# Upper products first, then lower ones, in each half chunk of a split fp32 matmul stream

## The reference

```python
proj  = rms_norm(x, ln_mix_pre) @ w_in            # 45 chunks of 128 output channels
x    += rms_norm(mixed @ w_out, ln_mix_post)      # 16
u     = conv(rms_norm(x, ln_ffn_pre) @ w_ffn_up)  # 4 x 22
f     = (gelu(gate) * up) @ w_ffn_down            # 4 x 16, over 11 tiles each
p     = rmsnorm(x, norm1_w) @ w_in_2              # 42
x    += mixed_2 @ w_out_2                         # 16
q     = rmsnorm(x, norm2_w) @ w_pq                # 16
act   = gelu(h @ u_tab.T) * gate_of_expert        # 8 x 16
x    += act @ v_tab                               # 8 x 16
```

## Time and profile before

| what | value |
|---|---|
| time, median of 3 runs | 4353.81 us (4353.56 to 4356.52) |
| profiled execution: its own time, its span | 4359.34 us, 4357.4 us |
| TensorE busy | 3741.0 us, 86% |
| VectorE busy | 2529.6 us, 58% |
| ScalarE busy | 1609.8 us, 37% |
| mean granted TensorE clock | 0.894 |
| data moved | 597.59 MB, mean 137 GB/s |

### The profile page before, as it was taken

The page is one execution under the profiler, slowest core; times in us unless marked ns, Lnnn a source line. Parts: engine busy times, 40 slices in busy tenths (PEclk is TensorE's granted clock), DMA queues, the critical chain, the costliest instruction groups (busy, mean ns, idle before and its releaser), DMA issues.

```text
span 4357.4 us, 73593 instructions
## 1 busy us (share of the span) xinstructions
PE 3741.0 (86%) x25038; PEld 3179.9 (73%) x25038; DVE 2529.6 (58%) x4253; ACT 1609.8 (37%) x2407; POOL 79.0 (2%) x80
## 2 busy tenths in 40 slices
PE   7996899999997977566766686379999999999998
PEld 5874778888886863455555575268888888888887
DVE  3465576767666753433233457976656566565565
ACT  3443344444443432211111232134445444354453
POOL 0000000000000000001000000000000000000000
PEclk8996999999998985667667797699999999999999
DMA  5550445555553530000000143146566565665654
GB/s 172 188 169 1 154 144 181 181 186 176 191 183 123 186 116 3 8 9 6 5 28 2 58 147 114 55 167 212 184 211 208 186 210 185 206 210 186 209 188 138
DMA packets 166055, 597.59 MB, mean 137 GB/s; under 512 B 18304, under 2 KB 26624, under 8 KB 164672
## 3 DMA queue, kind: packets, MB, share of 16 engines
q1 hardware_dynamic: 159456, 559.10, 39.1%
q0 software_dynamic: 6496, 36.96, 2.3%
HBM read 574.76 MB, written 20.97 MB: 137 GB/s over the span
## 4 chain that ended last, share of the span: by engine, by line
PE 81%; DVE 12%; issue 3%; ACT 2%; DMA 1%; DVEq 1%; SPq 0%; ACTq 0%; POOL 0%; POOLq 0%
PE bank L480 44%; PE bank L482 22%; PE bank L732 9%; PE bank L503 1%; DVE hot_row L1996 1%; PE bank L720 1%; PE bank L694 1%; DVE inv_T L1821 1%; DVE quad L1386 1%; PE bank L710 0%; PE bank L746 0%; DVE q_ms L1695 0%; DVE h_two L1376 0%; DVE rb L1371 0%; DVE inv_T L1807 0%
## 5 line engine op out<-in xcount | busy, mean ns | idle before, releaser
L480 PE MATMUL bank<-h_two,w_hi 128*128 128x512 f32 x5616 | 1974.5, 396 | 55.0 <-DVE h_two L1376 30.4
L482 PE MATMUL bank<-h_two,w_lo 128*128 128x256 f32 x5616 | 1582.2, 282 | 0.0
L1339 DVE TENSOR_TENSOR w_lo<-raw,w_hi 128x1024 fp32r<-128x1024 f32 (+1 forms) x1086 | 1262.4, 1186 | 98.7 <-ACT w_hi L968 94.7
L968 ACT ACTIVATE w_hi<-raw 128x1024 fp32r<-128x1024 f32 (+1 forms) x1086 | 1077.2, 1025 | 571.2 <-PE bank L482 496.7
L480 PEld LDWEIGHTS bank<-h_two,w_hi 128*128 128x128 f32 x5616 | 1060.3, 189 | 301.9 <-issue 38.2
L482 PEld LDWEIGHTS bank<-h_two,w_lo 128*128 128x128 f32 x5616 | 1071.3, 191 | 0.0
L480 PE MATMUL bank<-p_two,w_hi 128*128 128x512 f32 x2048 | 717.9, 393 | 0.0
L482 PE MATMUL bank<-p_two,w_lo 128*128 128x256 f32 x2048 | 572.5, 280 | 0.0
L480 PEld LDWEIGHTS bank<-p_two,w_hi 128*128 128x128 f32 x2048 | 383.8, 187 | 91.8
L482 PEld LDWEIGHTS bank<-p_two,w_lo 128*128 128x128 f32 x2048 | 384.2, 188 | 0.0
L973 ACT ACTIVATE stage<-bank 128x256 f32<-128x256 f32 x258 | 99.0, 384 | 581.2 <-PE bank L482 579.8
(11 more groups left out here) (329 smaller groups left out, 3202.1 us busy)
## 6 DMA issues: line engine op xcount, KB each, us to landing
raw<-in_u_tab SPq DMA_DIRECT2D x256, 512.0 KB, 4.2
raw<-in_v_tab SPq DMA_DIRECT2D x256, 512.0 KB, 4.5
raw<-in_w_up SPq DMA_DIRECT2D x176, 512.0 KB, 4.3
raw<-in_w_in SPq DMA_DIRECT2D x174, 512.0 KB, 4.5
raw<-in_w_out SPq DMA_DIRECT2D x64, 512.0 KB, 4.3
raw<-in_w_down SPq DMA_DIRECT2D x64, 512.0 KB, 3.5
raw<-in_w_pq SPq DMA_DIRECT2D x32, 512.0 KB, 4.7
gates<-g_stage POOLq DMA_DIRECT2D x8, 2048.0 KB, 7.5
```

What stands on the lines that cost most here:

```text
L480: nc.tensor.matmul(o[:], wh, two[:, k, :, :].rearrange("p a t -> p (a t)"), start=(k == 0), stop=False)
L482: last = nc.tensor.matmul(o[:, T:2 * T], wl, two[:, k, 0, :], start=False, stop=(k == nk - 1))
L968: nc.scalar.activation(w_hi[c % 2][:, at:end], raw[c % 2][:, at:end], ACT.Copy).then_inc(hi_done, 1)
L1339: nc.vector.tensor_tensor(w_lo[c % 2][:, at:end], raw[c % 2][:, at:end], w_hi[c % 2][:, at:end].bitcast(F32), ALU.subtract).then_inc(lo_do ...
```

## The change

In each half chunk the upper products of all its tiles come first, behind a wait for `hi_done` alone. The lower products of the same tiles follow, behind the wait for `lo_done`. `per_tile` is called ahead of the upper product. `half_done` is counted up by the last lower product of the half, as before. The number of products, their operands and the engines' other queues stay as they are.

```diff
-                for k in range(nk):
-                    if k * P in (0, HALF):
-                        pe.wait_ge(lo_done, it * 4 + (2 * c + 1 + k * P // HALF))
-                    if per_tile:
-                        per_tile(k)
-                    wh, wl = w_hi[c % 2][:, k * P:(k + 1) * P], w_lo[c % 2][:, k * P:(k + 1) * P]
-                    nc.tensor.matmul(o[:], wh, two[:, k, :, :].rearrange("p a t -> p (a t)"),
-                                     start=(k == 0), stop=False)
-                    last = nc.tensor.matmul(o[:, T:2 * T], wl, two[:, k, 0, :], start=False, stop=(k == nk - 1))
-                    if (k + 1) * P == HALF or k == nk - 1:
-                        last.then_inc(half_done, 1)
+                for part, ks in enumerate((range(HALF // P), range(HALF // P, nk))):
+
+                    pe.wait_ge(hi_done, it * 4 + (2 * c + 1 + part))
+                    for k in ks:
+                        if per_tile:
+                            per_tile(k)
+                        nc.tensor.matmul(o[:], w_hi[c % 2][:, k * P:(k + 1) * P],
+                                         two[:, k, :, :].rearrange("p a t -> p (a t)"), start=(k == 0), stop=False)
+                    pe.wait_ge(lo_done, it * 4 + (2 * c + 1 + part))
+                    for k in ks:
+                        last = nc.tensor.matmul(o[:, T:2 * T], w_lo[c % 2][:, k * P:(k + 1) * P], two[:, k, 0, :],
+                                                start=False, stop=(k == nk - 1))
+                    last.then_inc(half_done, 1)
```

## The result

| what | before | after |
|---|---|---|
| time, median (lowest to highest) | 4355.17 us (4353.56 to 4359.34, 4 runs) | 4384.73 us (4384.21 to 4386.45, 4 runs) |
| profiled execution: its own time, its span | 4359.34 us, 4357.4 us | 4384.72 us, 4382.7 us |
| mean granted TensorE clock | 0.894 | 0.892 |

The ratio is 1.0067, with a 95% interval of 1.0050 to 1.0085: slower, by 29.6 us on the medians and 25.4 us between the two profiled executions. The forecast was 4360 with a range of 4343 to 4405. That range held. The forecast's own one, 4355 to 4364, did not: the sign was as forecast, the size that of rival 1. By the forecast's own measure (8.7 us) this is slower, which it had given 0.38 against 0.46 for no change.

What follows compares the result with a forecast made beforehand. TensorE, busy 86% of the span, was taken as the bound, mostly by `chunk`'s products. Terms 6.4 + 0.9 + 0.5 + 0.5 + 0.4 - 2.4 = +6.3 us on the 4353.8 median gave 4360 us, range 4343 to 4405.

Steps and rivals of the forecast that it cites:

- rival 1: Pairs of `chunk` dearer in groups: 4407 if the slow rate rules, 4385 at 3 ns per lower; chance 0.26.
- No change of the products: Steady state of `chunk`: an upper and lower pair costs the same when eight uppers, then eight lowers follow; 0 us.
- The bounds (-226 and +611): All 8368 pairs: -226 us if 27 ns excess came from alternating, +611 if loads of 0.19 us paced lower runs.
- Rival 2: Pairs of `chunk` cheaper in groups: 4318 at 5 ns a pair, 4134 at all 27; chance 0.12.
- The two rates: Stages of `chunk` run at 0.3467 or about 0.353 us a pair; redrawn, all fast -8.6 us, all slow +47.
- The extra waits: Two more waits per chunk, 1086 in all, in TensorE's queue: 0 us taken, 35 us if uncovered.
- The `p_two` wait: First `p_two` chunk of 8 groups: eight lowers queue behind the wait at tile 15, 8 x 0.80 = +6.4 us.
- Rival 4: The `p_ready` loss at first `p_two` chunks does not come: 4353.7, no change; chance 0.12.
- `f_two`, `w_lo`: Two lowers stuck behind each of four `f_two` stops, +0.9 us; two `w_lo` waits let subtraction start earlier, -2.4 us.
- Rival 3: Waits for VectorE (`w_lo`) were the point: 4341.5 if all 12.3 us went and no `p_ready` loss came; chance 0.02.
- Stage starts: Lowers deferred behind `h_two` waits: first output +0.5, second output +0.5, FFN and second input +0.4 us together; query none.

Runs made afterwards that it cites:

- the split one: Changed kernel, but tile 15 taken alone in the second half of each group's first `p_two` chunk: 4376.77 us, against 4383.55 for the changed kernel.

## Why the prediction was off in size

**No change of the products, "I take 0 for this term": the step that failed.** Grouped pairs are dearer than the fast alternating ones: (2793 - 2773)/8 = 2.5 ns in `h_two` stages and (2827 - 2800)/8 = 3.4 ns in `p_two` ones. In the expert part that is the 10.7 us that the run with only steady chunks grouped shows. The bounds (-226 and +611) held it, and rival 1 had named its size (3 ns, 4385), but put it down to missed loads. The traces do not decide on that reason. Loads can come 0.11 us apart and lowers stand 0.120 apart, so missed loads alone do not give the number; but only those lowers are dearer whose own weights had no upper to load under, and at 384 columns the step is gone. That 4385 stands so near the measured 4384.73 is luck: it needs 25 us from dearer pairs, and the steady chunks of the two traces differ by 11.0 (10.3 + 8.3 - 5.1 - 2.5), since part of before ran at the slow rate. The first chunks differ by 14.4 (6.7 + 7.7) where the forecast had 6.3. Rival 2 is refuted: grouped pairs are not cheaper, and a product in a run of its kind keeps 13 to 17 ns above its columns (230 for 512 columns, 213 by the clock; only the first lower of a run has 7). By the Trainium skill ("TensorE: Matmul & The Clock Gate", section "Back-to-back issue gap") a pair would be 325 ns. The section gives this gap for an isolated product and says that a stream of loads and products is spaced otherwise. The grouped runs show 349, so its few nanoseconds do not hold here in either order.

**The two rates.** The prediction bounded this by -8.6 and +47 us. The changed kernel shows no second rate in the traces: all `h_two` stages run at 2793, between 2773 and 2827. So it lost 20 ns per half where before had been fast and won 34 where it had been slow. The slow rate may be why before scatters over 18 us (4347.15 to 4365.16 in 23 runs) and the changed kernel over 2 to 6; with one trace of before, that is not shown. The trace of the run with two waits and alternating products had the first input stage slow and the first output stage fast, the reverse of the trace of before, so it is not tied to a stage. The median loss of 29.6 us exceeds the 25.4 of the traces because the profiled execution of before was 4.2 us above its median.

**The extra waits.** 0 forecast, ratio 1.0002 measured, in the alternating order. Right.

**The `p_two` wait.** 8 x 0.80 = 6.4 us forecast. The first `p_two` chunk took 0.83 us more in each of 8 groups, 6.7 us, and taking tile 15 out of the group gave 6.8 us back. Right, by its mechanism as well: the profile counts the wait as 0.6 us (4.9 for 8) from the modelled end of upper 14, but upper 15 was due at 3183.07 + 7 x 0.23 = 3184.68 and started at 3185.48, 0.8 us later. The forecast's own terms add up to 3175.27 + 0.1 + 0.23 + 0.94 = 3176.54, 0.75 us late and not 0.80, a slip of 0.4 us in all. Rival 4 is out.

**`f_two`, `w_lo`.** `f_two` waits grew by 0.7 us, and the first down chunks by 0.65 in all, for 0.9 forecast; the subtraction's two waits shrank by 3.0 us for 2.4. Both right. Rival 3 is out.

**Stage starts.** +1.4 us forecast for the output, FFN and second input stages. Measured, with the work ahead of each, +1.4 (first output), +5.1 (FFN), +1.9 (second input), -2.1 (second output). The FFN start shows why. The windows of TensorE there, before and then after (us, busy and count, granted clock, DMA share, GB/s):

```profile
522.00:532.00 10.00, 7.01 (x32) 1.00 0.34 107
540.00:550.00 10.00, 8.86 (x32) 0.81 0.00 0
...
561.00:570.00 9.00, 8.46 (x48) 1.00 0.00 0
```

```profile
522.00:532.00 10.00, 9.57 (x31) 0.69 0.32 107
540.00:550.00 10.00, 6.09 (x17) 0.56 0.00 0
...
561.00:570.00 9.00, 8.29 (x25) 0.54 0.00 0
```

Two sets of 32 products for the sums of squares, which the change does not touch, took 10.05 us in place of 7.17 and then 9.56 in place of 8.86, the first at a granted clock of 0.69 where it had been 1.00. The first FFN chunk took 10.14 us in place of 8.58. 2.9 + 0.7 + 1.6 = 5.1 us: two thirds lie outside the edit. The first chunk's part, 1.6 us, fits the forecast's remark that the clock can stay low where uppers alone leave gaps, which it priced at 1.5 us but left out of the sum (+0.4 for two such starts). The first set took 7.17 to 8.86 us in the three traces that alternate throughout, 9.81 in groups of 4, 10.16 in groups of 2, and 9.85 to 10.05 in the two of the changed kernel and the split one's. But it took 8.66 with the first chunks alternating and all others grouped, and 7.17 where the first of every pair was grouped. Whether the order of products moves the clock, or the clock merely fell at another moment, was not settled.

**What stays open.** Why a grouped pair costs 2.5 to 3.4 ns more, why groups of 4 are dearer than groups of 8, and what picks one of two rates for a whole stage. The second wait and late operands are excluded by the runs above. Loads that are nearly as long as the lower products are not. No order tried beat the kernel before: alternating with both waits equals it, groups of 2 come within 0.11%.

## What to carry to other kernels

Before relaxing a wait, read what it costs in total. Here the `w_lo` wait was 12.3 us in two places, and the order that relaxed it touched 8368 products, of which one nanosecond each is 8.4 us. Work deferred behind a later wait is paid for when that wait is live: an operand that arrives for the last tile wants everything else done before it, so split the last tile off. And an isolation edit keyed to a hook (`per_tile`) must be checked against the loops: here it also hit every second chunk of five kinds of stage, and only those where it did not, the expert part above all, could be read.

## What the runs showed of the hardware

- A product in a run of its kind costs its columns at 2.4 GHz and 13 to 17 ns: 230 ns for 512 columns, 176 for 384, 120 for 256. The first product of 256 columns behind a run of 512 costs 113; alternating with products of 512, it is 117.
- Weight loads of 128 x 128 follow each other at 0.11 us and set the pace of narrower products in a run: 0.84 us for eight of 128 columns, 0.87 for eight of 192. Alternating with products of 512 columns, halving 256 to 128 took 7 ns off a pair of 347.
- The same alternating code holds 2773 or 2827 ns per half for a whole stage, at a granted clock of 1.00, and the difference is in the products of 512 columns alone (230 or 236.5 ns); grouped in eights the `h_two` stages had one value, 2793. `p_two` stages are 27 to 34 ns dearer per half than `h_two` ones in both orders.
- Alternating and grouped chunks in turn gave 2814 to 2815 ns, worse than either alone at its best.
- The granted clock of untouched products moved from 1.00 to 0.69 after a stall of the same length (3.41 us in both traces).
